# The first gate and up pair of both FFNs multiplied plainly in a macaron decoder layer, with the operand sums of the seven-product form made on DVE beside it

## What is computed

```python
x += 0.5 * swiglu(rmsnorm(x, ffn1_norm), ffn1_w_gate, ffn1_w_up, ffn1_w_down)
x += mixer(rmsnorm(x, mix_norm))            # stick-breaking attention and causal pooling
x += cross_attention(rmsnorm(x, mem_q_norm), rmsnorm(mem, mem_kv_norm))
x += 0.5 * swiglu(rmsnorm(x, ffn2_norm), ffn2_w_gate, ffn2_w_up, ffn2_w_down)
y = rmsnorm(x, final_norm)
swiglu(h, wg, wu, wd) = (silu(h @ wg) * (h @ wu)) @ wd
```

## Time and profile before

| | |
|---|---|
| median of 3 runs | 2162.31 us |
| the profiled execution, its own time | 2162.35 us |
| its span, first to last instruction | 2160.6 us |
| PE, DVE, ACT, POOL busy | 93%, 66%, 42%, 33% of the span |
| mean granted TensorE clock | 0.965 of full speed |

### The profile page before, as it was taken

How to read it: one execution, slowest core, us unless ns; L and a number is a source line. 1 busy time by engine, 2 the same in 40 slices (tenths; PEclk the granted TensorE clock), 3 DMA queues, 4 the chain that set the end, 5 groups by cost and what they waited for, 6 DMA issues and landing times. The chain is left out here.

```text
span 2160.6 us, 26117 instructions
## 1 busy us (share of the span) xinstructions
PE 2015.9 (93%) x9585; PEld 1679.5 (78%) x9585; DVE 1428.6 (66%) x1921; ACT 904.2 (42%) x1606; POOL 723.4 (33%) x602
## 2 busy tenths in 40 slices
PE   4899999999999999877889999994999999999997
PEld 3688888887887689666778888883888888887886
DVE  7756556559798532599955565567656565569896
ACT  6443443434445212566633444443443433334443
POOL 3655545530003021388711100124645555520000
PEclk7899999999999999899899999996999999999999
DMA  3222223244300221432134432230223222264201
GB/s 118 73 83 69 88 83 93 78 179 170 138 20 6 87 89 59 108 78 59 48 91 126 136 88 59 60 108 0 79 83 93 79 82 87 75 239 151 78 1 79
DMA packets 217496, 190.21 MB, mean 88 GB/s; under 512 B 7532, under 2 KB 173976, under 8 KB 217368
## 3 DMA queue, kind: packets, MB, share of 16 engines
q1 hardware_dynamic: 217280, 188.51, 28.2%
q10 hardware_dynamic: 88, 0.02, 0.0%
HBM read 152.85 MB, written 35.65 MB: 87 GB/s over the span
## 5 line engine op out<-in xcount | busy, mean ns | idle before, releaser
L1731 DVE TENSOR_TENSOR w_lo<-st,w_hi 128x512 fp32r<-128x512 f32 x176 | 192.7, 1095 | 200.6 <-ACT w_hi L1321 200.4
L928 PE MATMUL ps<-T_hi,w_lo 128*128 128x512 f32 x704 | 278.4, 395 | 48.4 <-DVE T_lo L1731 47.7
L929 PE MATMUL ps<-T_lo,w_hi 128*128 128x512 f32 x704 | 276.6, 393 | 0.0
L930 PE MATMUL ps<-T_hi,w_hi 128*128 128x512 f32 x704 | 276.4, 393 | 0.0
L928 PE MATMUL ps<-tr_hi,sr_lo 128*128 128x512 f32 x616 | 242.6, 394 | 5.1 <-DVE xT L1920 2.7
L930 PE MATMUL ps<-tr_hi,sr_hi 128*128 128x512 f32 x616 | 240.5, 390 | 0.0
L929 PE MATMUL ps<-tr_lo,sr_hi 128*128 128x512 f32 x616 | 240.3, 390 | 0.0
L928 PE MATMUL ps<-B_hi,w_lo 128*128 128x512 f32 x528 | 207.7, 393 | 8.5 <-DVE w_lo L1731 6.1
L929 PE MATMUL ps<-B_lo,w_hi 128*128 128x512 f32 x528 | 207.3, 393 | 0.0
L930 PE MATMUL ps<-B_hi,w_hi 128*128 128x512 f32 x528 | 207.1, 392 | 0.0
L928 PEld LDWEIGHTS ps<-T_hi,w_lo 128*128 128x128 f32 x704 | 133.6, 190 | 82.6 <-DVE T_lo L1731 33.9
(11 more groups left out here) (236 smaller groups left out, 4752.5 us busy)
## 6 DMA issues: line engine op xcount, KB each, us to landing
gate_raw<-in_ffn_w_gate SPq DMA_DIRECT2D x44, 512.0 KB, 5.3
up_raw<-in_ffn_w_up SPq DMA_DIRECT2D x44, 512.0 KB, 5.1
h_spill<-up_s SPq DMA_DIRECT2D x66, 256.0 KB, 2.0
piece_A<-in_ffn_w_down SPq DMA_DIRECT2D x32, 512.0 KB, 4.5
piece_B<-h_spill SPq DMA_DIRECT2D x32, 512.0 KB, 6.0
wa_raw<-in_w_in SPq DMA_DIRECT2D x16, 512.0 KB, 4.0
wb_raw<-in_w_out SPq DMA_DIRECT2D x16, 512.0 KB, 4.1
wb_raw<-in_mem_w_kv SPq DMA_DIRECT2D x16, 512.0 KB, 3.9
```

Source lines behind the costliest of these rows:

```text
L928: pe.matmul(to, w_lo, m_hi, start=first, stop=False, skip_group_check=joins)
L929: pe.matmul(to, w_hi, m_lo, start=False, stop=False, skip_group_check=joins)
L930: return pe.matmul(to, w_hi, m_hi, start=False, stop=last, skip_group_check=joins)
L1731: return dve.tensor_tensor(to, value, plain(hi), ALU.subtract)
```

## The change

m = 0 and 1 of each FFN (the first gate and the first up pair) are computed with 8 plain block products each. Their order on TensorE, in `first_pair`: gate with the first token half, chunk by chunk as the normalized tiles come; then up with the first half; then gate and up with B12; then gate and up with B22. The seven-product form begins at m = 2, in the order 1, 6, 7, 2, 5, 4, 3. The left blocks of the pair are split straight from the loaded weights (`first_hi`, `first_lo`), four per matrix. B12 and B22 get whole buffers of their own (`b_keep[1]`, `b12_hi`, `b12_lo`, over memory of T1, T4 and the rows of x). T1 to T4 are all made on DVE, in `entry`, from the kept tiles, with temporaries laid over the up weights and over buffers for results. `x_turns` takes the chunks in their natural order.

```diff
-            def right_sums(r, c):        # POOL
...
+            def first_pair(r):           # PE
...
+                pe.wait_ge(c_wlo, 8 * r + 4)
+                for d in range(DC):
+                    pe.wait_ge(s_xn, DC * NTH[6 * r] + d + 1)
+                    for i in range(2):
+                        mm = chunk(0, 0, i, d, d == 0, d == DC - 1)
...
+                    if r == 0 and d == 5:
+                        x_turns(0, 4)
+                    elif r == 1 and d == 2:
+                        norm_tot(7)
+                    elif r == 1 and d == 5:
+                        norm_bc(7)
+                if r == 0:
...
+                    norm_bc(1)
+                    x_turns(4, DC)
+                    pe.wait_ge(s_xt_a, HT + DC)
...
+                pe.wait_ge(c_wlo, 8 * r + 8)
+                for i in range(2):
+                    for d in range(DC):
+                        mm = chunk(1, 0, i, d, d == 0, d == DC - 1)
+                    mm.then_inc(c_done, 1)
+                for which in range(2):
+                    for i in range(2):
...
+                        for c in range(QC):
+                            pe.wait_ge(t_blo, 8 * r + c + 1)
+                            mm = chunk(which, 1, i, c, c == 0, False)
+                        mm.then_inc(c_prod, 1)
+                for which in range(2):
+                    for i in range(2):
+                        for c in range(QC):
+                            pe.wait_ge(t_blo, 8 * r + QC + c + 1)
+                            mm = chunk(which, 1, i, QC + c, False, c == QC - 1)
+                        mm.then_inc(c_done, 1)
...
             def ffn(r):                  # PE
-                product(r, 0, 1)
...
-                for m in range(NM):
-                    for p in seq(m):
-                        if m or p not in (1, 2):
-                            product(r, m, p)
+                first_pair(r)
+                for m in range(2, NM):
+                    for p in ORDER:
+                        product(r, m, p)
...
+            def right_hi(r, c, k):       # ACT
+                act.wait_ge(t_sum, 16 * r + 4 * c + 4)
+                if k == "T4":
+                    act.wait_ge(c_prod, 4 * (r + 1))
+                copy(t_hi[k][:, c, :], t_tmp[c % 2][k][:]).then_inc(t_thi, 1)
...
+            def right_sums(r, c):        # DVE
+                n, tmp = 16 * r + 4 * c, t_tmp[c % 2]
...
+                if c == 0:
+                    dve.wait_ge(c_wlo, 8 * (r + 1))
+                    dve.wait_ge(t_b, 8 * (r + 1))
+                elif c == 1:
+                    dve.wait_ge(p1_store[1], 16 * (PAIRS * r + 1))
+                else:
+                    dve.wait_ge(t_tlo, 16 * r + 4 * (c - 1))
+                dve.tensor_tensor(tmp["T1"][:], b12, b11, ALU.subtract).then_inc(t_sum, 1)
+                dve.tensor_tensor(tmp["T3"][:], b22, b12, ALU.subtract).then_inc(t_sum, 1)
...
+                dve.tensor_tensor(tmp["T2"][:], b22, tmp["T1"][:], ALU.subtract).then_inc(t_sum, 1)
...
+                dve.tensor_tensor(tmp["T4"][:], b21, tmp["T2"][:], ALU.subtract).then_inc(t_sum, 1)
...
+            def entry(r):                # DVE
+                second(r)
+                hidden(r, 0, "c11")
+                hidden(r, 0, "c21")
+                right_sums(r, 0)
+                right_sums(r, 1)
+                for c in range(QC):
+                    for k in TSPLIT:
+                        if (c, k) == (0, "T4"):
+                            weight_lo(r, 2, 1)
+                        right_lo(r, c, k)
+                    if c + 2 < QC:
+                        right_sums(r, c + 2)
+                    if c == 2:
+                        weight_lo(r, 2, 6)
+                        weight_lo(r, 2, 7)
+                hidden(r, 0, "c12")
+                hidden(r, 0, "c22")
+                for p in (2, 5, 4, 3):
+                    weight_lo(r, 2, p)
...
             def ffn_loads(r):            # SP
+                sp.wait_ge(c_wlo, 8 * r + 4)
+                raw_load(r, 2)
+                store(r, 0, "c11")
+                store(r, 0, "c21")
+                sp.wait_ge(t_tlo, 16 * (r + 1))
+                raw_load(r, 3)
+                store(r, 0, "c12")
+                store(r, 0, "c22")
```

More of the change, by code:

```diff
@@ L919, in _ @@
                     sum_squares(q, c)
-            for p in (5, 6, 7):
-                left_sum(1, 0, p)
             ffn(1)
@@ new lines, in second_hi @@
+            def second_hi(r, n):
+                act.wait_ge(t_b, 8 * r + n + 1)
+                to = b12_hi if n < QC else t_hi["B22"]
+                copy(to[:, n % QC, :], b_keep[1][:, n, :]).then_inc(t_bhi, 1)
+            def right_hi(r, c, k):
[4 more added lines that the diff above has]
+            def entry(r):
+                silu(r, 0, "c11")
+                silu(r, 0, "c21")
+                for n in range(DC):
+                    second_hi(r, n)
+                for c in range(QC):
+                    for k in TSPLIT:
+                        if (c, k) == (0, "T4"):
+                            act.wait_ge(c_prod, 4 * r + 1)
+                            weight_hi(r, 2, 1)
+                        right_hi(r, c, k)
+                    if c == 2:
+                        silu(r, 0, "c12")
+                        weight_hi(r, 2, 6)
+                        weight_hi(r, 2, 7)
+                        silu(r, 0, "c22")
+                act.wait_ge(c_done, nth_first(r, 0, 1, 1))
+                weight_hi(r, 2, 2)
+                weight_hi(r, 2, 5)
+                act.wait_ge(c_done, nth_first(r, 1, 1, 0))
+                weight_hi(r, 2, 4)
+                weight_hi(r, 2, 3)
@@ L1406, in ffn @@
             def ffn(r, behind):
-                for m in range(NM):
+                for m in range(2, NM):
                     t = m // 2
-                    for p in seq(m):
-                        if m == 0 and p in (1, 2):
-                            continue
+                    for p in ORDER:
                         if p == 1:
@@ L1467, in _ @@
                     row_square(HT + (1, 3, 5, 6).index(c))
-            weight_hi(0, 0, 6)
-            weight_hi(0, 0, 7)
-            copy_out(0, 0, 1, "s1")
             norm_std(1)
-            for n in range(6):
+            for n in range(DC):
                 x_copy(n)
-            silu(0, 0, "c11")
-            act.wait_ge(s_xt_ps, 2 * DC)
-            for c in range(QC):
-                if c < 2:
-                    x_copy(6 + c)
-                right_hi(0, c)
-            act.wait_ge(t_tlo, 5 * QC)
-            for p in (5, 4, 3):
-                weight_hi(0, 0, p)
+            first_hi(0, 1)
+            entry(0)
             def a_weight(n):
@@ L1686, in _ @@
                         copy(a_hi_t[half][:, HD * h + e, :], ps[:, 4 + (k + e) % 4, :]).then_inc(b_ehi, 1)
-            weight_hi(1, 0, 6)
-            weight_hi(1, 0, 7)
-            copy_out(1, 0, 1, "s1")
+            act.wait_ge(b_out, n_units)
+            first_hi(1, 1)
             norm_std(7)
-            silu(1, 0, "c11")
-            for c in range(QC):
-                right_hi(1, c)
-            act.wait_ge(t_tlo, 10 * QC)
-            for p in (5, 4, 3):
-                weight_hi(1, 0, p)
+            entry(1)
             def row_mean(t):
```

274 lines of the change are left out of this document (144 added, 130 removed).

## The result

| | us |
|---|---|
| before, beside the change (4 runs) | 2161.97 (2160.55 to 2162.58) |
| the change (4 runs) | 2111.36 (2107.66 to 2114.07) |
| ratio | 0.9771, 95% interval 0.9759 to 0.9783 |
| the profiled execution of the change | 2112.14, span 2110.1, mean clock 0.981 |

The change is faster by 50.6 us. The forecast was 2115.7, the range 2110 to 2124.

What follows compares the result with a forecast made beforehand. TensorE's stream and its holes, chiefly 47.7 us of T_lo waits at the FFN entries, were taken as the bound. Gains of 17.6 and 29.0 sum to 46.6, so 2162.35 becomes 2115.7 us, range 2110 to 2124.

Steps and rivals of the forecast that it cites:

- Start, 22.1: First FFN: two more gate splits on DVE, 1.2 us, make TensorE start at 22.1 rather than 20.9.
- Gate and transposes: First FFN: 48 gate matmuls, 12 of them slow, take 13.3 us; after transposes and norm spreading TensorE is through at 40.8.
- The new stall: First FFN, ahead of up: TensorE stands 3.1 us for ACT's last x copy and up splits and DVE's last `lo`.
- The clock falls, 1.6 us: First FFN, start of up: the clock falls in the stall, 8 or 9 slow matmuls cost 1.6 us; other end 0.
- B12 and B22 in time, second half 21.8: First FFN: DVE makes the B12 and B22 tiles by 56.0, so 96 second-half products take 21.8 us without waiting.
- The T4 split waits for the B12 products: First FFN, DVE: T4 lies over B12's splits, so its split waits until 67.6 and an ACT copy, 68.9.
- Waits in m = 2: Product 7 waits 0.1 to 0.3 us for c22, product 2 waits 1.2 for ACT's s1 copy; m = 2 is 1.4 late.
- First FFN 17.6: First FFN: m = 2 begins in effect at 79.9 rather than 97.47, 17.6 us gained.
- Second FFN 29.0: Second FFN: m = 2 begins in effect at 1516.2 against 1545.17, 29.0 us gained, with 1.0 of wait allowed at the norm.
- that the wait moves to products 6 and 7: Rival, m = 2: the T wait only moves there, 6.5 us per FFN, 13 in all, 2128.7; chance 0.14.
- That the clock holds and small waits vanish: Rival: the clock holds through the transposes and the small waits vanish, 5.4 us less, 2110.3; chance 0.12.
- a clock that never rises: Rival, plain pair: all 192 matmuls run at 0.427 us, making the kernel slower at 2188; chance 0.02.

Runs made afterwards that it cites:

- the run with the gap of 0.84: The changed kernel, with ACT splitting the first FFN's four up blocks after four of its eight x copies instead of all eight: 2108.44 us.
- ACT's and POOL's order mended: The changed kernel with three edits: up splits after four x copies, POOL's left sums after the second FFN's norm diagonals, ACT's s1 copy before a weight split: 2103.17 us.
- the run with 24 more: The changed kernel with up's block product with B22 computed twice in each FFN, 24 matmuls more; only its time is used: 2117.04 us.
- the one with POOL behind the norm: The changed kernel, with POOL in the second FFN starting m = 2's left sums only after DVE has written the norm's diagonals: 2109.64 us.
- s1 first: The changed kernel, with ACT's copy of the s1 result of m = 2 ahead of the split of the third weight sum: 2111.48 us.

## Why the prediction was right, and where not

- **What bounds the kernel, and cover by plain products: right.** 47.7 us of `T_lo` waits are gone, and the runs with the sums on the other engine show that cover does most of it (38.8 of 48.1 us).
- **24 matmuls more, fully on the path: right**, shown by doing it once more: 3.6 us net per FFN, 5.4 less the waits that it fills.
- **Start, 22.1: wrong by 3.2 us**, the largest error. The step added two splits to the start of before and did not ask what else leaves that place: POOL's left sums do, so DVE's norm steps take 0.16 and 0.87 in place of 1.18 and 2.96. The prediction counted POOL's left sums where they now are, and not where they had been.
- **Gate and transposes**: with that start, TensorE was to be through at 37.6 and was at 37.0; twelve slow matmuls, as said. (Over the other versions with the plain pair their number was 7 to 14.)
- **The new stall: right in place and cause, 3.98 for 3.1.** TensorE was through with its transposes sooner than I took it, while ACT's copies and splits set the end.
- **The clock falls, 1.6 us: right.** The stretch 41.6 to 44.6 held some eight slow matmuls, 1.7 us against a full stream from 41.01 on; the other end of the range, 0, is what the run with the gap of 0.84 shows. That transposes do not count as busy in the same way as other matmuls (the Trainium skill, TensorE: Matmul & The Clock Gate, Part 4) agrees with it, but no run here separates them from the gap: the run with the early splits has the same sixteen transposes ahead of a gap of 0.84 and keeps the clock.
- **B12 and B22 in time, second half 21.8: right**, 53.6 to 75.36 without a hole.
- **The T4 split waits for the B12 products: right**, 3.38 us of idle DVE for 2.5. The consequence I drew from it too late: since the chain hangs there on TensorE, moving TensorE earlier moves the chain as well.
- **Waits in m = 2**: product 7 0.18 (forecast 0.1 to 0.3), product 2 1.16 (1.2). Right, but each stop sets the stream back by about 0.2 us more than the idle time shown: 1.86 in all instead of 1.4.
- **First FFN 17.6, measured 20.25**: the start's 3.2 sooner, less 0.5 in m = 2.
- **Second FFN 29.0, measured 27.9**: m = 2 began 47.2 after the first gate matmul instead of 46.6, for the norm waited 1.57 where 1.0 was allowed, and m = 2 lost 0.5 more. The contention of `lo` with POOL was named, but priced at 0.68 to 1.2 each; they took 1.6 (6.45 / 4).
- **Sum** 46.6 for 48.1. That it is so near is in part luck: the first FFN was 2.7 too low and the second 1.1 too high. The median fell by 50.6; in the profile 2.4 come from stretches outside the entries, which no term of the prediction held.
- **Rivals**: that the wait moves to products 6 and 7 did not happen, and with the sums on POOL it does, at 3.7 per FFN; the 6.5 was priced for 24 DVE instructions behind the T4 split, all slow, and with the sums on POOL DVE has 16 there, seven of them slow. That the clock holds and small waits vanish did not happen here; with ACT's and POOL's order mended it largely does, 2103.17, the earlier start included. Nothing was seen of a clock that never rises; but that every dense stretch rises within 5 us is too narrow: the first twelve gate matmuls of the kernel before took 5.3 us, and 14 slow ones behind the gap took 6 (from 40.28 to 46.4 in the run with 24 more).

## What to carry over

Work that needs no late operand, put between an operand's raw form and its first user, can be worth nearly the chain's full wait even where it costs instructions: 48 matmuls bought 39 us by themselves and 46 with the sums on DVE. When a change moves one engine's work, ask which work on *another* engine it uncovers at the old place and disturbs at the new one: that was the largest error here, and both cheap gains behind it (4.4 and 1.9 us) were orders on ACT and POOL. Holding an engine back can move the contention rather than remove it, so look at where its work goes. Add small gains only with a run of the sum: an edit that was to remove 0.4 us of wait moved a load by 1.2 and cost over 2.

## What was not expected of the hardware

- A DVE step on 128x4 values takes 0.16 alone and 1.18 when it meets a POOL addition; four diagonals 0.87 and 2.96.
- The granted clock after a gap is not a function of the gap alone to within a matmul: after the same 3.98 us it was full for the first two or three matmuls in four profiles (the change, its two repeats and the one with POOL behind the norm; up began at 41.0 to 41.1), and low from the first in three (sums on POOL, 24 more matmuls, s1 first; up began at 40.2 to 40.5). The same three had only 7 slow matmuls at the start of the gate, the four had 12 or 13; behind the gap they had 14 where the four had 8 or so. Both kinds come to about 20 in all, so the mark hardly differs. Why one profile takes the one way and one the other is open.
- Each stop of TensorE at full clock sets the stream back by 0.2 us more than the idle time shown. Of it 0.16 is how the rows are to be read: idle time counts from the modelled end of a matmul, 0.39 after its start, while in a full stream the next one starts after 0.227. The rest is that the matmul behind the first one follows after 0.30 instead of 0.23.
